# The mixer's feature-major products as matmuls of 512 columns over both parts of the operand

## The reference

```python
def hybrid_mixer(x, norm_g, w_in, gdn_conv_w, a_log, dt_bias, ...):
    h = rmsnorm_2(x, norm_g)
    proj = h @ w_in                       # 2048 x 7184
    qkv_a, z_a, b_a, a_a, qkv_b = ...     # 3 x 1024, 1024, 8, 8, 3 x 1024
    qkv_a = silu(causal_dwconv_2(qkv_a, gdn_conv_w))   # 4 taps over the tokens
    o_a = gated_delta_rule(l2norm(q_a), l2norm(k_a), v_a, g, beta)
    o_b = moba_attention(q_b, k_b, v_b, rel_bias)      # 256 tokens: one block
    ...
    return o @ w_out
```

## Time and profile before

| | |
|---|---|
| median of three runs | 2522.6 us (2519.57 to 2526.09) |
| profiled execution | 2520.34 us, span 2519.0 us |
| PE busy | 2447.4 us, 97% |
| PE weight loads busy | 2189.5 us, 87% |
| DVE busy | 1647.1 us, 65% |
| ACT busy | 1119.0 us, 44% |
| POOL busy | 260.3 us, 10% |
| mean granted TensorE clock | 0.986 of 2.4 GHz |

### The profile page before, as it was taken

One profiled execution on the slowest core, in us unless ns is written; L12 is line 12 of the kernel. 1 busy time (PEld: TensorE's weight loads), 2 busy tenths in 40 slices (PEclk: granted clock), 3 DMA queues, 4 the chain that ended last, 5 costly groups with the idle time before them and its releaser, 6 DMA issues.

```text
span 2519.0 us, 36758 instructions
## 1 busy us (share of the span) xinstructions
PE 2447.4 (97%) x14956; PEld 2189.5 (87%) x14956; DVE 1647.1 (65%) x2274; ACT 1119.0 (44%) x1477; POOL 260.3 (10%) x129
## 2 busy tenths in 40 slices
PE   8999999999999999989999999997999999999997
PEld 7888699888888888879898998897888888888886
DVE  4999766666666666777646443354776776767677
ACT  4000445544554454455436345554544444444443
POOL 0000000000000000023333333330010000000000
PEclk9999999999999999999899999998999999999998
DMA  7445556666666666555334355462565656565653
GB/s 234 153 145 169 162 188 193 192 186 191 193 187 190 193 191 187 188 157 152 98 101 116 96 149 146 156 193 91 181 190 189 192 188 189 192 190 188 191 192 118
DMA packets 377575, 428.05 MB, mean 170 GB/s; under 512 B 16408, under 2 KB 323904, under 8 KB 377408
## 3 DMA queue, kind: packets, MB, share of 16 engines
q1 hardware_dynamic: 372288, 421.58, 53.6%
q10 hardware_dynamic: 5120, 4.12, 0.6%
HBM read 423.54 MB, written 3.67 MB: 170 GB/s over the span
## 4 chain that ended last, share of the span: by engine, by line
PE 93%; DVE 3%; ACT 3%; issue 1%; DMA 0%; POOL 0%; ACTq 0%; DVEq 0%
PE product L562 37%; PE product L511 20%; PE product L564 19%; PE product L536 10%; PE product L533 1%; ACT w_hi L463 1%; PE small L1677 1%; PE small L1691 1%; PE small L1687 1%; DVE delta_work L1914 0%; DVE w_lo L470 0%; DVE x_residual L619 0%; PE small L1634 0%; PE small L898 0%; PE small L1730 0%
## 5 line engine op out<-in xcount | busy, mean ns | idle before, releaser
L470 DVE TENSOR_TENSOR w_lo<-w_raw,w_hi 128x1024 fp32r<-128x1024 f32 x640 | 796.0, 1247 | 516.5 <-ACT w_hi L463 515.8
L463 ACT ACTIVATE w_hi<-w_raw 128x1024 fp32r<-128x1024 f32 x712 | 750.4, 1058 | 854.6 <-PE product L564 569.5
L562 PE MATMUL product<-h_operand,w_hi 128*128 128x512 f32 x2432 | 846.0, 393 | 4.7 <-DVE x_residual L765 4.7
L564 PE MATMUL product<-h_operand,w_lo 128*128 128x256 f32 x2432 | 677.5, 279 | 0.0
L562 PEld LDWEIGHTS product<-h_operand,w_hi 128*128 128x128 f32 x2432 | 456.2, 188 | 108.7 <-DVE x_residual L765 5.0
L564 PEld LDWEIGHTS product<-h_operand,w_lo 128*128 128x128 f32 x2432 | 458.5, 189 | 0.1
L562 PE MATMUL product<-mlp_hidden,w_hi 128*128 128x512 f32 x1024 | 355.7, 394 | 0.9 <-DVE x_residual L619 0.8
L478 POOL TENSOR_TENSOR w_lo<-w_raw,w_hi 128x1024 fp32r<-128x1024 f32 x72 | 181.9, 2527 | 1435.5 <-ACT w_hi L463 1435.5
L564 PE MATMUL product<-mlp_hidden,w_lo 128*128 128x256 f32 x1024 | 283.7, 277 | 0.0
L511 PE MATMUL product<-h_operand,w_hi 128*128 128x256 f32 x1408 | 266.7, 291 | 5.0 <-POOL w_lo L478 3.3
L562 PE MATMUL product<-mid_operand,w_hi 128*128 128x512 f32 x704 | 244.3, 390 | 0.0
(11 more groups left out here) (289 smaller groups left out, 2550.1 us busy)
## 6 DMA issues: line engine op xcount, KB each, us to landing
w_raw<-in_mlp_w SPq DMA_DIRECT2D x256, 512.0 KB, 3.8
w_raw<-in_w_in SPq DMA_DIRECT2D x112, 512.0 KB, 3.7
w_raw<-in_w_gate SPq DMA_DIRECT2D x88, 512.0 KB, 3.5
w_raw<-in_w_up SPq DMA_DIRECT2D x88, 512.0 KB, 4.0
w_raw<-in_w_down SPq DMA_DIRECT2D x88, 512.0 KB, 3.2
w_raw<-in_cc_w_in SPq DMA_DIRECT2D x128, 256.0 KB, 2.9
w_raw<-in_cc_w_out SPq DMA_DIRECT2D x32, 512.0 KB, 4.8
w_raw<-in_w_out SPq DMA_DIRECT2D x32, 512.0 KB, 4.2
```

What stands on the lines that cost most here:

```text
L463: act.activation(k.w_hi[i % SPLIT], k.w_raw[i % RAW], ACT.Copy).then_inc(*k.act_done.mark("w_hi", i))
L470: dve.tensor_tensor(k.w_lo[i % SPLIT], k.w_raw[i % RAW], k.w_hi[i % SPLIT].bitcast(F32), ALU.subtract).then_inc(*k.dve_done.mark("w_lo", i))
L562: pe.matmul(out, hi[:, kk, n], x.both[:, kt].rearrange("p a t -> p (a t)"), start=s == 0 and kk == 0, stop=False, skip_group_check=True)
L564: done = pe.matmul(out[:, 0:T], lo[:, kk, n], x.hi[:, kt, :], start=False, stop=last and kk == WIDE_K - 1, skip_group_check=True)
```

## The change

The six w_in products of parts 0 to 2 and the moba blocks 0 to 3, which come out by features, go from `pe_product` to `pe_wide_product`. Their weights are loaded in slots of 512 rows by 256 features; the number and size of the slots and the turns between DVE and POOL stay. The very first product runs `in_turn`. Each half is evicted at its last slot in three instructions: ACT copies the first row of sums, DVE adds the second, DVE multiplies by the norm's row in place. The first half of a product is therefore written at its fourth slot (its seventh in the in-turn one), and ACT waits there until the taps of the product before have read `pad`. The taps still begin after the second half.

```diff
--- before.py
+++ after.py
@@ -365,14 +365,15 @@
             self.slots[key] = range(first, len(self.parts))
             self.on_pool += [pool and i % pool == 0 for i in self.slots[key]]
 
-        def wide(key, name, col, k0=0, n=D, in_turn=False):
-            steps, rows = [], range(k0, k0 + n, WIDE_K * P)
+        def wide(key, name, col, k0=0, n=D, in_turn=False, pool=0):
+            first, steps, rows = len(self.parts), [], range(k0, k0 + n, WIDE_K * P)
             for s, half in [(s, half) for s in range(len(rows)) for half in range(2)] if in_turn else [
                     (s, half) for half in range(2) for s in range(len(rows))]:
                 steps.append((half, s, len(self.parts)))
                 c = col + half * PAIR
                 self.parts.append([d[name][rows[s]:rows[s] + WIDE_K * P, c:c + PAIR].rearrange("(k p) n -> p k n", p=P)])
-                self.on_pool.append(False)
+                self.on_pool.append(pool and steps[-1][2] % pool == 0)
+            self.slots[key] = range(first, len(self.parts))
             self.order[key] = [(half, s, i, s == len(rows) - 1) for half, s, i in steps]
 
         for b in range(D // PAIR):
@@ -396,9 +397,9 @@
                     wide(("w2", c, b), "mlp_w2", b * COLS, c * MLP_CHUNK, MLP_CHUNK)
         for g in range(2):
             for part in range(3):
-                product(("w_in", part, g), "w_in_2", part * GW + g * COLS, 2)
+                wide(("w_in", part, g), "w_in_2", part * GW + g * COLS, in_turn=g == part == 0, pool=2)
         for b in MOBA_BLOCKS:
-            product(("moba", b), "w_in_2", 4 * GW + 2 * NG + b * COLS, 2)
+            (product if b >= 4 else wide)(("moba", b), "w_in_2", 4 * GW + 2 * NG + b * COLS, pool=2)
         for g in range(2):
             product(("w_in", 3, g), "w_in_2", 3 * GW + g * COLS, 2)
         for half, b in W_OUT_ORDER:
@@ -2224,11 +2225,14 @@
         for part in range(3):
             if g == 0 and part == 1:
                 k.pe_beside.start(pe_gates(k, pe))
-            pe_product(k, pe, ("w_in", part, g), k.h, ready)
+            pe_wide_product(k, pe, ("w_in", part, g), k.h, ready)
             if part == 2:
                 k.pe_beside.start(turn_v(g))
     for b in MOBA_BLOCKS:
-        pe_product(k, pe, ("moba", b), k.h, ready, tokens_out=b >= 4)
+        if b >= 4:
+            pe_product(k, pe, ("moba", b), k.h, ready, tokens_out=True)
+        else:
+            pe_wide_product(k, pe, ("moba", b), k.h, ready)
     for g in range(2):
         pe_product(k, pe, ("w_in", 3, g), k.h, ready, tokens_out=True)
         if g:
@@ -2268,6 +2272,17 @@
             k.bank.give(("v turned", g, t), k.act_done)
         yield
 
+    def first_padded_row(g, part, half):
+        if g or part:
+            act.wait_ge(*k.dve_done.at("taps", *((g, part - 1) if part else (g - 1, 2))))
+        else:
+            act.wait_ge(*k.pool_done.at("pad zeros"))
+        act_first_row(k, act, k.pad[:, half * PT:(half + 1) * PT, GDN_K - 1:], ("w_in", part, g), half)
+
+    def first_moba_row(b, half):
+        act.wait_ge(*k.pe_done.at("inter", b % 2, NCH - 1))
+        act_first_row(k, act, (k.mq, k.mk)[b // 2][b % 2][:, half * PT:(half + 1) * PT, :], ("moba", b), half)
+
     def z_block(g):
         psum = k.acc.at(("w_in", 3, g))
         act.wait_ge(*k.pe_done.at("w_in", 3, g))
@@ -2307,12 +2322,15 @@
         for part in range(3):
             if g == 0 and part == 1:
                 k.act_beside.start(act_gates(k, act))
-            act_product(k, act, ("w_in", part, g))
+            act_wide_product(k, act, ("w_in", part, g), lambda half: first_padded_row(g, part, half))
             k.act_beside.start(after(4, silu(g, part, (k.q_t, k.k_t, k.z)[part][g])))
             if part == 2:
                 k.act_beside.start(after(TURN_AFTER - 1, turn_v(g)))
     for b in MOBA_BLOCKS:
-        act_product(k, act, ("moba", b), (lambda: copy_tokens(b)) if b >= 4 else None)
+        if b >= 4:
+            act_product(k, act, ("moba", b), lambda: copy_tokens(b))
+        else:
+            act_wide_product(k, act, ("moba", b), lambda half: first_moba_row(b, half))
     for g in range(2):
         act_product(k, act, ("w_in", 3, g), lambda: z_block(g))
         if g:
@@ -2347,21 +2365,20 @@
                 k.dve_done.note("taps", g, part)
             yield
 
-    def padded(g, part):
-        key = ("w_in", part, g)
-        dve.wait_ge(*k.pe_done.at(*key))
-        if g or part:
-            dve.wait_ge(*k.dve_done.last())
-        dve_times_row(k, dve, "mix_norm", k.pad[:, :, GDN_K - 1:], k.acc.at(key), "padded", g, part)
-        k.acc.give((key,), k.dve_done)
-        k.dve_beside.start(taps(g, part, (k.q_t, k.k_t, k.z)[part][g]))
-
-    def copy_out(b):
-        dst, g = (k.mq, k.mk)[b // 2][b % 2], b % 2
-        dve.wait_ge(*k.pe_done.at("moba", b))
-        dve.wait_ge(*k.pe_done.at("inter", g, NCH - 1))
-        dve_times_row(k, dve, "mix_norm", dst, k.acc.at(("moba", b)), "moba", b)
-        k.acc.give((("moba", b),), k.dve_done)
+    def times_row(out, key, half, *name):
+        dve_second_row(k, dve, out, key, half)
+        dve.wait_ge(*k.dve_done.at("row", "mix_norm"))
+        dve.wait_ge(*k.dve_done.at("rows added", *key, half))
+        dve.tensor_tensor(out, out, spread_row(k.row["mix_norm"], PT), ALU.mult).then_inc(*k.dve_done.mark(*name))
+        k.dve_done.note("applied", "mix_norm")
+
+    def padded(g, part, half):
+        times_row(k.pad[:, half * PT:(half + 1) * PT, GDN_K - 1:], ("w_in", part, g), half, "padded", g, part)
+        if half:
+            k.dve_beside.start(taps(g, part, (k.q_t, k.k_t, k.z)[part][g]))
+
+    def copy_out(b, half):
+        times_row((k.mq, k.mk)[b // 2][b % 2][:, half * PT:(half + 1) * PT, :], ("moba", b), half, "moba", b)
 
     def gated(g):
         dve.wait_ge(*k.act_done.at("z", g))
@@ -2382,9 +2399,12 @@
         for part in range(3):
             if g == 0 and part == 1:
                 k.dve_beside.start(dve_gates(k, dve))
-            dve_product(k, dve, ("w_in", part, g), lambda: padded(g, part))
+            dve_wide_product(k, dve, ("w_in", part, g), lambda half: padded(g, part, half))
     for b in MOBA_BLOCKS:
-        dve_product(k, dve, ("moba", b), (lambda: copy_out(b)) if b < 4 else None)
+        if b >= 4:
+            dve_product(k, dve, ("moba", b))
+        else:
+            dve_wide_product(k, dve, ("moba", b), lambda half: copy_out(b, half))
     for g in range(2):
         dve_product(k, dve, ("w_in", 3, g))
         if g:
```

## The result

The changed kernel takes 2527.3 us (median of 20 runs, 2524.3 to 2531.5) beside 2522.1 for the kernel before (20 runs); the ratio is 1.0022, 95% interval 1.0015 to 1.0029. It is 5.5 us slower by the ratio. The forecast was 2518.0, 4.6 us faster. The time lies inside the stated range of 2511 to 2529, but the kernel moved the other way; it is where rival 4 stood (2523 to 2528, given 7%). Three executions in the sets behind this text, of 2723, 2907 and 4942 us, were far slower than the others of their kernels and enter no ratio.

What follows compares the result with a forecast made beforehand. PE was taken to bound the kernel. Savings of 8.6 us less 0.2, 0.4, 0.8, 1.9, 0.5 and 0.2 left 4.6 us, so 2518.0 against the median of 2522.6; the 8-in-10 range was 2511 to 2529.

Steps and rivals of the forecast that it cites:

- rival 4: One more PE wait of 5 to 10 us, not found (in-turn accumulators or lock): 2523 to 2528 us, 7%.
- what bounds it now: PE bounds the kernel, 93% of the last-ending chain; time PE does not need is saved unless PE then waits.
- what is not kept: Losses taken off the 8.6 us matmul saving: 0.2, 0.4, 0.8, 1.9, 0.5 and 0.2 us.
- Chains (0.5): At PE's waits on gates, delta rule and norms, some five shorter slots only lengthen the wait: 0.5 us lost.
- Eviction: Ten products' evictions add 12 us on ACT, 15 on DVE, hidden in idle time; 0.2 us lost at block 2.
- Matmuls (8.6 us): Ten changed products: 640 places, each a pair of 346.5 ns instead of a 360.0 ns triple, saving 8.6 us.
- pairs at 350 ns or more: Sign that would show the forecast wrong; it expected pairs of 346 to 347 ns in the mixer.
- Half clock (0.2): Slot 24 and about as much behind 1123.37 us run at half clock and save nothing: 0.2 us less.
- Start (0.4): Slots 0 to 3: slot 1 waits 3.3 us, hidden because slot 4 awaits POOL's w_lo; their 0.4 us saving is lost.
- Slots 17 to 24 (0.8 + 1.9): ACT waits for the taps: slots 17 to 23 lose their 0.8 us saving, late squares cost PE 1.9 us.
- rival 2: ACT's wait for the taps starves PE at two of five w_in boundaries, clock falling behind: 2533 us, 15%.

Runs made afterwards that it cites:

- the mended one: Changed kernel with w_ba_lo one slot earlier, w_in products evicted into a separate stage buffer, w_lo of moba blocks 1 and 3 on DVE alone: 2515.2 us, 0.9968 to before.
- the last experiment: Against the mended one: each 512-column matmul of the w_in and moba products split into two of 256; 2523.6 us, 1.0006 to the kernel before.
- the narrow form with the same two mends: Kernel before, all products narrow, with w_ba_lo one slot earlier and w_lo of moba blocks 1 and 3 on DVE alone: 2520.1 us, 0.9993 to before.

## Why the prediction was wrong

*The chain of argument "what bounds it now" held.* PE bounds the mixer. The forecast failed in the sum's second part, what is not kept: it had 4.0 us there, and the traces show some 12.8. The steps that failed are "Chains (0.5)", which let no chain start later, and "Eviction", whose work was "hidden" with 0.2 us for block 2. The clock, 4.4 of the 12.8, had a term only at the start. The saving too was smaller, 5 to 7 us for 8.6.

*Matmuls (8.6 us).* The mechanism is right, the size is not. 640 matmuls fewer are worth an estimated 5.6 us by the 22 slots, in the kernel with the waits and in the mended one alike, some 6 at equal clock, and 9.6 (5.9 to 13.3) by the ratios. The cadence is less simple than 346.5 ns. PE of the changed kernel at 1163 and at 1176 us, the first of a run of pairs and the one 13 pairs on, then the same with 27:

```profile
1163.33 0.40 PE L563 MATMUL product<-h_operand,w_hi 128*128 128x512 f32 x1
...
1167.85 0.39 PE L563 MATMUL product<-h_operand,w_hi 128*128 128x512 f32 x1
```

```profile
1176.44 0.40 PE L563 MATMUL product<-h_operand,w_hi 128*128 128x512 f32 x1
...
1185.98 0.40 PE L563 MATMUL product<-h_operand,w_hi 128*128 128x512 f32 x1
```

4.52 / 13 = 347.7 ns, and 9.54 / 27 = 353.3 ns. Long runs of pairs go at one or the other and change over where other work of PE or a spell at half clock lies between. Against 360.0 that is 12.3 and 6.7 ns a place, between 4.3 and 7.9 us over 640. The words "pairs at 350 ns or more" were to show the prediction wrong; in a part of the slots they did. Why there are two levels is open. So the term by cadence is 4 to 8 us.

*Half clock (0.2).* It was said that nothing is saved there. Right: pairs at the lower clock start 0.64 us apart, and so do three narrow matmuls. PE's narrow matmuls of slot 24 in the kernel before start 0.213 us apart from 1197.0 to 1201.7, 0.64 for three.

*Start (0.4).* Right: a wait of 3.1 us, and slot 4, behind POOL's w_lo, began at 1122.4, 18.0 us behind slot 0 as before, with nothing lost.

*Slots 17 to 24 (0.8 + 1.9).* Right in place, waiter and order of events; 3.4 us in the traces and 4.3 (1.5 to 7.1) by removing it. The part left out is the clock: it was at half longer than before, and the matmuls behind the wait took 1.8 us more.

*Chains (0.5).* This is the step that failed first. It said that shorter slots inside a chain only lengthen PE's wait on it. It didn't ask whether the chain itself would start later. Ahead of slot 11 PE had become 2.8 us earlier, and DVE's queue had four eviction instructions in place of one and two more stretched ones just before w_ba_lo, which came 1.4 us later: a wait that was not there, 3.0 us, and its clock, 1.7. Removing it gave 5.8 (3.0 to 8.6).

*Eviction and lock (10 us of DVE, "hidden but at slot 19"; 0.2 for block 2).* The DVE total was right (+ 24.7 us in the mixer: 346.6 beside 321.9; ACT + 9.2). "Hidden" was wrong, three times: at slot 11, at block 2 (2.0 us for 0.2) and at the first head. Stretching by POOL was counted for the added products only. But earlier slots and later DVE also move old instructions into POOL's time: at L2127 by about a microsecond, and 0.17 us became 1.85. Removing that gave 5.8 us (3.1 to 8.5), 3.3 of it in the trace at that place.

*Which operations POOL holds up.* The prediction spoke only of DVE instructions with two inputs in SBUF. The rows of L2127 show that a TENSOR_SCALAR on 128 x 2 numbers is held too, 1.85 us beside 0.17. The Trainium skill (SBUF — State Buffer, "Who interferes with whom") names tensor_scalar among the operations that can take the shared ports in a two-port mode, when its operands meet the conditions of that mode, and so be blocked whole; these rows agree. The prediction had quoted the other half of that rule. And the rule of the Trainium skill on the fixed cost of a matmul (TensorE: Matmul & The Clock Gate, "Wait — 56ns, not 53.3ns?"), about 2.5 ns, would make the last experiment's 640 matmuls an estimated 1.6 us. The trace does not agree, 8.8 ns a matmul in the 22 slots beside its 2.5, and neither do the runs, 9.6 us and at least 5.9.

*Rivals.* Rival 4 (one more wait that was not found, the lock named among its causes) and rival 2 (two bad places at w_in boundaries) each describe a part. What happened is four places. Three were each taken away by itself: the taps 4.3, the gates' weights 5.8, the lock 5.8, or 13.6 us all at once. The fourth, block 2's eviction with some 2.0 us, stands in the traces and was not taken away by an experiment. In rival 2 only one of the two places was ACT's wait; the other was DVE's own queue. That each fall of the clock comes from the wait ahead of it is shown where both went together (slot 11, the first head); at slot 24 the kernel before had half clock without the wait.

## What to carry to other kernels

When an eviction is cut in pieces and moved forward, list every small operation that stands behind it on the same engine, and follow the one that PE will ask for next. Slack of the engine as a whole (DVE was idle a third of the time) says nothing about it. Price each new wait of PE of 2 to 3 us with the slower matmuls behind it, here 1.5 to 1.8 us each. Compare the granted clock of two kernels before their times: 0.002 of it is 5 us here, as much as the whole change. Then mend before judging: the form that lost 5.5 us was 6 to 8 under the kernel before when one small operation came a slot earlier, and eight w_lo and (for the last 2 us) an eviction had another place; beside the narrow form with the same two mends it was 4.5 (give or take 3.2).

## What the runs showed that was not expected

- The pairs of one operand have two cadences, 346 to 348 and 353.3 ns, each for many slots on end.
- A DVE operation on 128 x 2 numbers took 0.17 us, or 1.85 when it began 0.55 us into a GpSimd instruction of 2.38 us.
- Three new or longer waits of PE, of 2.0 to 3.0 us, were followed by half clock where the kernel before had none: 7.44 us for 5.69, 5.07 for 3.61, pairs at 0.64 us for 0.35. In the kernel before a wait of 1.8 us at the second of these places had full clock behind it.
- The same 640 matmuls cost nothing measurable by the ratios (-0.3, give or take 3.3) in the changed kernel and 9.6 us (give or take 3.7) in the mended one. In 22 slots at equal clock they cost the same in both, 8.8 ns each.
